# Modulation pieces of a linear-attention layer as VectorE row sums, gate logits ahead of one projection unit, and the next block's low part ahead of the norm's root

## The reference

```
m = einsum('bd,de->be', silu(c), w_ada) + b_ada          # 6 x 1024 values per layer and group
sh1, sc1, gt1, sh2, sc2, gt2 = split(m, 6)
h = rms_norm(x, norm) * (1 + sc1) + sh1
x = x + gt1 * gla_mixer(h)        # q, k, v, r, gate logits -> chunkwise state -> out
x = x + gt2 * conv_ffn(rms_norm(x, norm) * (1 + sc2) + sh2)
```

## Time and profile before

| | us |
|---|---|
| median of 3 runs (lowest, highest) | 1480.11 (1478.75, 1481.41) |
| the profiled execution | 1480.64 |
| its span | 1478.9 |
| TensorE busy | 1426.8 (96%) |
| VectorE busy | 830.7 (56%) |
| ScalarE busy | 644.9 (44%) |
| mean granted TensorE clock | 0.994 |

### The profile page before, as it was taken

One profiled execution on the slowest core, in us unless ns is written; L12 is line 12 of the kernel. 1 busy time (PEld: TensorE's weight loads), 2 busy tenths in 40 slices (PEclk: granted clock), 3 DMA queues, 4 the chain that ended last, 5 costly groups with the idle time before them and its releaser, 6 DMA issues.

```text
span 1478.9 us, 27109 instructions
## 1 busy us (share of the span) xinstructions
PE 1426.8 (96%) x11464; PEld 1328.3 (90%) x11464; DVE 830.7 (56%) x1332; ACT 644.9 (44%) x1427; POOL 78.9 (5%) x122
## 2 busy tenths in 40 slices
PE   4999999999999999999989999999899999999999
PEld 2877788899999999999978887878799999999999
DVE  4533442537776866868654455465675555455454
ACT  4423433436555245243354655553455552452431
POOL 0000000030000000000210000000200000000000
PEclk9999999999999999999999999999999999999999
DMA  9233242253333533534532232212512222223222
GB/s 376 92 140 124 88 154 93 93 200 115 114 115 103 183 121 109 172 121 152 215 118 87 74 100 74 65 49 77 200 58 86 86 72 100 86 72 103 84 74 103
DMA packets 34074, 171.87 MB, mean 116 GB/s; under 512 B 3857, under 2 KB 6033, under 8 KB 22050
## 3 DMA queue, kind: packets, MB, share of 16 engines
q1 hardware_dynamic: 21330, 118.49, 22.7%
q0 software_dynamic: 12624, 51.66, 9.5%
HBM read 162.22 MB, written 7.91 MB: 115 GB/s over the span
## 4 chain that ended last, share of the span: by engine, by line
PE 91%; DVE 4%; ACT 2%; issue 1%; DMA 1%; POOL 1%; POOLq 0%; SPq 0%; DVEq 0%; ACTq 0%
PE ps L548 27%; PE ps L550 26%; PE ps L549 26%; PE ps L649 1%; PE ps L921 1%; PE ps L963 1%; DVE w_lo L1432 1%; PE ps L586 1%; DVE h_lo L1481 1%; PE ps L876 1%; POOL acc L481 1%; DVE sq L1474 1%; PE ps L656 1%; ACT w_hi L1022 1%; PE ps L941 1%
## 5 line engine op out<-in xcount | busy, mean ns | idle before, releaser
L548 PE MATMUL ps<-h_hi,w_hi 128*128 128x272 f32 x2080 | 609.5, 293 | 12.4 <-DVE h_lo L1481 10.3
L550 PE MATMUL ps<-h_hi,w_lo 128*128 128x272 f32 x2080 | 603.4, 290 | 0.0
L549 PE MATMUL ps<-h_lo,w_hi 128*128 128x272 f32 x2080 | 600.4, 289 | 0.0
L548 PEld LDWEIGHTS ps<-h_hi,w_hi 128*128 128x128 f32 x2080 | 393.2, 189 | 24.6 <-issue 12.7
L549 PEld LDWEIGHTS ps<-h_lo,w_hi 128*128 128x128 f32 x2080 | 394.0, 189 | 1.2 <-issue 1.2
L550 PEld LDWEIGHTS ps<-h_hi,w_lo 128*128 128x128 f32 x2080 | 392.8, 189 | 0.0
L1432 DVE TENSOR_TENSOR w_lo<-w_raw,w_hi 128x2048 fp32r<-128x2048 f32 (+2 forms) x109 | 227.1, 2083 | 113.7 <-ACT w_hi L1022 113.5
L1022 ACT CAST w_hi<-w_raw 128x2048 fp32r<-128x2048 f32 (+2 forms) x109 | 188.2, 1727 | 217.2 <-PE ps L550 182.4
L549 PE MATMUL ps<-act_lo,w_hi 128*128 128x272 f32 (+1 forms) x704 | 204.1, 290 | 0.0
L548 PE MATMUL ps<-act_hi,w_hi 128*128 128x272 f32 (+1 forms) x704 | 203.6, 289 | 0.0
L550 PE MATMUL ps<-act_hi,w_lo 128*128 128x272 f32 (+1 forms) x704 | 203.4, 289 | 0.0
(11 more groups left out here) (250 smaller groups left out, 1612.1 us busy)
## 6 DMA issues: line engine op xcount, KB each, us to landing
w_raw<-in_wst SPq DMA_DIRECT2D x73, 1024.0 KB, 4.8
w_raw<-in_wst SPq DMA_DIRECT2D x28, 768.0 KB, 4.1
a_raw<-in_ada_r POOLq DMA_DIRECT2D x32, 512.5 KB, 3.7
a_raw<-in_ada_w POOLq DMA_DIRECT2D x24, 512.0 KB, 5.0
a_gap<-in_ada_w POOLq DMA_DIRECT2D x12, 1024.0 KB, 8.6
a_pro<-in_ada_w SPq DMA_DIRECT2D x8, 1024.0 KB, 18.5
w_raw<-in_wst SPq DMA_DIRECT2D x8, 512.0 KB, 3.7
xT<-in_xT SPq DMA_DIRECT2D x4, 544.0 KB, 7.7
```

The lines of the kernel that those rows point to most:

```text
L548: mm(out, lhs_hi, rhs_hi, start=first, stop=False)
L549: mm(out, lhs_hi, rhs_lo, start=False, stop=False)
L550: return mm(out, lhs_lo, rhs_hi, start=False, stop=last)
```

## The change

Five things change.

1. The pieces 8 to 19 become row sums: 48 instructions of 128 x 1024 on VectorE, twelve in each head slot, placed by the table `GLA_ROWS` (its entry says how many follow the units of a fill step). The 12 products on TensorE, the 12 copies on ScalarE, the 12 selections and the 12 additions go. One addition of all biases (`gla_biases`) comes at the end of the last slot. GpSimd loads rows (`ada_g`, the same bytes, a half at a time, each after the row sums that last read that half) and, once, the two rows of `c` spread over the partitions into `a_part` and `sq`; ScalarE applies silu to them, with a table load before and after.
2. `GLA_STEPS` has seven steps: one unit moves from before the gate logits to between the logits and the second pair of states. In the first and the last slot the step ahead of `turn_outputs` has one unit in place of two.
3. ScalarE squares a head's output in place in PSUM, after its copy, so that `sq` is free.
4. At the three boundary norms, `low` of the next block stands ahead of the wait for the root.
5. There, the product of the fourth piece moves from before the first chunk to after the second, into bank 6 in place of 7; the copy of the third piece waits for it as well.

```diff
@@ head slots on TensorE @@
-                rider = 8 + 3 * h
+                def fill(step):
+                    units([next(todo) for _ in range(GLA_STEPS[h][step])])
                 fill(0)
                 keys_and_scores(h)
                 fill(1)
-                ada_mm(rider)
                 state_terms(h, 0)
-                fill(2, rider)
-                ada_mm(rider + 1)
+                fill(2)
                 ...
-                fill(3, rider + 1)
+                fill(3)
                 ...
                 gate_logits(h + 1)
-                ada_mm(rider + 2)
+                fill(4)
                 state_terms(h, 1)
@@ tables @@
-GLA_STEPS = [[1, 3, 2, 1, 1, 1], [1, 3, 2, 2, 2, 3], [1, 3, 2, 2, 2, 3], [1, 3, 2, 1, 0, 1]]
+GLA_STEPS = [[1, 3, 1, 1, 1, 1, 1], [1, 3, 2, 1, 1, 2, 3], [1, 3, 2, 1, 1, 2, 3], [1, 3, 1, 1, 1, 0, 1]]
+GLA_ROWS = [[0, 3, 3, 0, 2, 2, 2], [1, 3, 2, 0, 2, 2, 2], [1, 3, 2, 0, 2, 2, 2], [2, 3, 3, 0, 2, 2, 0]]
@@ head slots on VectorE @@
+                def fill(step_):
+                    rows = GLA_ROWS[h][step_]
+                    for _ in range(GLA_STEPS[h][step_]):
+                        evacuate(next(todo), not (h == GH - 1 and step_ == 6))
+                        if rows:
+                            ada_rows()
+                            rows -= 1
+                    for _ in range(rows):
+                        ada_rows()
@@ one row sum @@
+                gla = m < GLA_ROWS_DONE
+                x = a_raw[:, t, 0:D] if gla else a_raw[:, t, :]
+                c = c_gla[grp] if gla else c_row[:, grp, :]
+                STT(out=prod_gla if gla else a_prod[:, :], in0=x, scalar=1.0, in1=c, op0=ALU.mult, op1=ALU.mult,
                     accum_out=ada[:, l, 2 * b + t, grp:grp + 1]).then_inc(arow_ok, 1)
+            def gla_biases():
+                dve.wait_ge(arow_ok, GLA_ROWS_DONE)
+                TT(ada[:, 0, t, :], ada[:, 0, t, :], b_ada[...], ALU.add).then_inc(bias_ok, 1)
@@ loads, on GpSimd @@
+                    if n < len(GLA_RIDERS):
+                        pool.dma_start(a_raw[:, t, 0:D], A["ada_g"][n, t]).then_inc(a_in[t], 16)
@@ ScalarE, an output of a head @@
-                A_(sq[0:m, 0, 0:DV], ps[0:m, b, 0:DV], ACT.Square, accum_out=o_ss[0:m, r:r + 1])
-                act.copy(o_rows[0:m, r, :], ps[0:m, b, 0:DV]).then_inc(o_out, 1)
+                act.copy(o_rows[0:m, r, :], ps[0:m, b, 0:DV])
+                A_(ps[0:m, b, 0:DV], ps[0:m, b, 0:DV], ACT.Square, accum_out=o_ss[0:m, r:r + 1]).then_inc(o_out, 1)
@@ ScalarE, before the first slot @@
+            act.wait_ge(crow_in, 32)
+            for grp in range(2):
+                A_(c_gla[grp], c_gla[grp], ACT.Silu).then_inc(crow_ok, 1)
+            act.preload_act_table_set(LNEXP)
@@ a boundary norm, VectorE @@
             def norm(which, n_ada):
                 make_gain(which, (0, KT), n_ada)
+                low(BN[{1: ("up", 0, 0, 1), 2: ("dq", 0), 3: ("up", 1, 0, 1)}[which]])
                 dve.wait_ge(rstd_ok, which + 1)
                 ...
                     modulated_lo(which, k)
-                    if k == 3:
-                        low(BN[{1: ("up", 0, 0, 1), 2: ("dq", 0), 3: ("up", 1, 0, 1)}[which]])
@@ a boundary norm, TensorE @@
                 ada_mm(riders[2])
-                ada_mm(riders[3])
 
             def first_after(which, name, stage):
-                first_block(name, stage, range(0, 6))
+                first_block(name, stage, range(0, 2))
+                ada_mm(riders[3])
+                first_block(name, stage, range(2, 6))
```

More of the change, by code:

```diff
@@ L54 @@
 GAP_RIDERS = {1: list(range(20, 24)), 2: list(range(40, 44)), 3: list(range(44, 48))}
-RAW_NO = {i: n for n, i in enumerate(GLA_RIDERS + FFN_RIDERS)}
+ROW_RIDERS = GLA_RIDERS + FFN_RIDERS
 GAP_NO = {i: n for n, i in enumerate(GAP_RIDERS[1] + GAP_RIDERS[2] + GAP_RIDERS[3])}
-ROWS_DONE = 4 * len(FFN_RIDERS)
+GLA_ROWS_DONE, ROWS_DONE = 4 * len(GLA_RIDERS), 4 * len(ROW_RIDERS)
 DC = D + 1
-ada_count = lambda i: i + 1 if i < FFN_RIDERS[0] else i + 1 - len(FFN_RIDERS)
+ada_count = lambda i: i + 1 - sum(j <= i for j in ROW_RIDERS)
+GLA_ROWS = [[0, 3, 3, 0, 2, 2, 2], [1, 3, 2, 0, 2, 2, 2], [1, 3, 2, 0, 2, 2, 2], [2, 3, 3, 0, 2, 2, 0]]
 VEC = {}
@@ L457, in _ @@
             pool.memset(eps[:, :], EPS).then_inc(const_ok, 1)
[L459 to L465, removed]
             def row_load(n):
@@ L504, in gap_loads @@
                     pool.dma_start(a_gap[:, GAP_NO[i] % 4, :, :], A["ada_w"][l, b].rearrange("p (k c) -> p k c", c=BC)).then_inc(a_gap_in[GAP_NO[i] % 4], 16)
-            for i in GLA_RIDERS:
-                rider_load(i)
+            pool.wait_ge(ada_mm_ok, 6)
+            row_load(0)
+            pool.wait_ge(ada_sel_ok, 8)
+            pool.wait_ge(h_ok, KT)
+            for grp in range(2):
+                pool.dma_start(c_gla[grp], A["c_row"][grp:grp + 1].partition_broadcast(P)).then_inc(crow_in, 16)
+            for n in range(1, len(GLA_RIDERS)):
+                row_load(n)
             pool.wait_ge(h_ok, 2 * KT)
@@ L512, in _ @@
             sum_tiles(1)
-            pool.wait_ge(ada_mm_ok, GAP_RIDERS[1][-1] + 1)
+            pool.wait_ge(ada_mm_ok, ada_count(GAP_RIDERS[1][-1]))
             pool.dma_start(c_row[:, :, 0:D], A["c_row"].partition_broadcast(P)).then_inc(crow_in, 16)
             pool.memset(c_row[:, :, D:DC], 1.0).then_inc(crow_one, 1)
-            for n in range(len(FFN_RIDERS)):
+            for n in range(len(GLA_RIDERS), len(ROW_RIDERS)):
                 row_load(n)
@@ L628, in ada_mm @@
                     src = lambda k: a_pro[:, i, k, :]
-                elif i in GAP_NO:
+                else:
                     pe.wait_ge(a_gap_in[GAP_NO[i] % 4], 16 * (GAP_NO[i] // 4 + 1))
                     src = lambda k: a_gap[:, GAP_NO[i] % 4, k, :]
[L632 to L635, removed]
                 if i in GAP_NO:
@@ L1052, in part @@
             def part(i):
-                act.wait_ge(ada_mm_ok, ada_count(i))
+                act.wait_ge(ada_mm_ok, ada_count(i) + (1 if i in GAP_NO and GAP_NO[i] % 4 == 2 else 0))
                 if i >= 4:
@@ L1169, in gla_slot @@
                     act.preload_act_table_set(LNEXP)
-                part(rider)
                 fill(2)
-                part(rider + 1)
                 fill(3)
                 gates(h + 1)
-                part(rider + 2)
+                fill(4)
                 outputs_out(h, 0, 6)
@@ L1462, in make_gain @@
                 dve.wait_ge(ada_ok, ada_count(n_ada - 1))
-                if which >= 2:
-                    dve.wait_ge(arow_ok, ROWS_DONE)
+                if which:
+                    dve.wait_ge(arow_ok, ROWS_DONE if which >= 2 else GLA_ROWS_DONE)
+                if which == 1:
+                    dve.wait_ge(bias_ok, 1)
                 k0, k1 = ks
@@ L1662, in gla_slot @@
                 todo = iter(fill_units(h))
-                rider = 8 + 3 * h
-                def fill(step_, piece=None):
-                    n = GLA_STEPS[h][step_]
-                    for i in range(n):
-                        evacuate(next(todo))
-                        if piece is not None and i == (n - 1 if step_ == 4 else 0):
-                            ada_add(piece)
-                    if piece is not None and n == 0:
-                        ada_add(piece)
+                def fill(step_):
[7 more added lines that the diff above has]
+                        ada_rows()
                 fill(0)
@@ L1690, in gla_slot @@
                 else:
-                    evacuate(next(todo), False)
+                    fill(6)
+                    gla_biases()
                     output_lo(oT, 1, 0)
@@ L1959, in _layout @@
     A["ada_r"] = rows
+    A["ada_g"] = np.stack([f("w_ada")[0][:, i * BC:(i + 1) * BC].T.reshape(2, P, D) for i in GLA_RIDERS])
     vec = np.zeros((P, NVEC), np.float32)
```

48 lines of the change are left out of this document (27 added, 21 removed).

## The result

The changed kernel takes 1462.9 us in the median of four runs (1459.7 to 1464.9), against 1480.2 for the kernel before (four runs, one more than in the table above). The ratio is 0.988, with a 95% interval of 0.986 to 0.990: 17.3 us faster, well beyond the 3 us that can be told from nothing. The forecast was 1464.8. The profiled execution took 1464.41 us (span 1462.5), against 1480.64 before.

A forecast was written before the change was run, and what follows sets the result against it. TensorE was taken to bound the kernel (91% of the chain). 24.7 removed - 9.85 waits - 3.0 clock + 3.5 norms = 15.3 us off 1480.64: 1465.3 profiled, 1464.8 as median; range 1454 to 1470.

The forecast's parts named there:

- Removed, 24.7: Linear-attention part, TensorE: products 12.0, selections 5.4, idle time 5.8 and slow clock after the first slot's hole 1.5 us go.
- The 1.7 us ahead of the outputs: TensorE's idle time before the outputs, waiting for VectorE's `bb`; claimed to go because a projection unit now covers it.
- Waits, 9.85: New TensorE waits for VectorE's queue across the four head slots: 4.35 + 0.2 + 4.4 + 0.9 us.
- The two of 0.1: Second and third slot, TensorE's wait for the gated output: 0.1 us counted in each.
- The 0.9 us of the first slot: First slot's new TensorE waits: 0.15 us at the third v unit, 0.75 at the second states.
- rival (a): VectorE gets through its stream earlier, so the new linear-attention waits don't form: 1452 us; chance 0.13.
- Clock, 3.0: Slow clock behind new linear-attention holes: 1.5 us for the 4.35 us hole, half that for each of two of 2.2.
- Rival (c): TensorE's clock stays at 2.4 GHz through the new holes; 3.0 and 2.5 us come back: 1459 us; chance 0.18.
- Norms, 3.5: Three boundary norms: net gain of 0.6 + 2.2 + 0.7 us from the earlier low part, slow stretches charged.
- Row sums, 1.22: VectorE's time per new row sum, from the profile's row for 1025 elements; 1.25 us taken with its semaphore.
- rival (b): A row sum takes 2.44 us in the head slots: +24 us, 1489, slower than before; chance 0.04.
- Rival (d): Row-sum loads are late, at 7.6 us: 2.1 us more in the first slot, about 1 later: 1468 us; chance 0.15.

## Why the prediction was right

The profiled time was foretold as 1465.3 and came as 1464.41; 1.6 us of the difference to before is the wait for the first inputs, so that the change itself gave 14.6 where the sum said 15.3. By the medians it gave 17.3, 1462.9 for 1464.8. The mechanism was right at the places that carry the sum (work removed, waits and their releasers, slow stretches behind them), but the closeness of the sum is luck in part: in the profiled execution the waits came 1.85 us shorter and the clock cost some 2 more, and at the norms two wrong sizes cancel.

**Removed, 24.7.** The stage lost 11.4 us while it took on 8.0 of holes and 4.7 of slow clock: 24.1 were removed. The total was right; one term had the wrong label. The 1.7 us ahead of the outputs is not what the moved logits are worth. The product that stood there had covered part of VectorE's gates, and without it the old order has waits of 0.6, 1.85 and 1.85, one of 1.1 at a v unit of the first slot, 0.3 more, and slow stretches: 8.9 us in all. The prediction compared with a state in which both edits were made, so the error in the label did no harm.

**Waits, 9.85.** The gated output: 4.35 walked, 4.21 measured. The third v unit: 2.2 walked, 1.91 measured, twice, with the releaser named. The two of 0.1 are not in the trace. The 0.9 us of the first slot didn't appear: the gate logits' unit, the second states (L758 at 96.34) and the v units follow one another there without a wait. Sum 8.0. This was the boldest part and carried rival (a) away: the moved row sums show that exactly these waits, and nothing else of 60 us of new VectorE work, stood on the path.

**Clock, 3.0.** 4.7 in the profiled execution, where all three holes were followed by a slow stretch. But this was chance in part: with the same holes, five other executions kept full speed behind both of 1.91 us, and lost (1 - clock) x 8 us = 1.7 to 2.5 behind the one of 4.2. The changed kernel's own runs show it too: the fastest, 1459.7 us, had a mean clock of 0.994, the others (1461.4, 1464.4, 1464.9) 0.991; 1461.4 and 1464.9 at one clock show that not all of the spread is the clock's. So the term is 2 to 5 us, and 3.0 was a mean of things that either happen or don't, which I had read off two holes of 2.08 us. Rival (c) is half true: it held for ten of twelve holes of 1.91 us, and not for the long one in any of six executions. The spare matmuls show, for the holes at the norms, that the hole causes the slow stretch: with them it is absent six times of six, without them it is there 17 times of 18.

**Norms, 3.5.** 3.3 measured. The split by edit, 0.6, 2.2 and 0.7, was as well: 0.6, 1.95 and 0.7. The second norm's share rests on a slow stretch that the execution of before had by chance; with the edit undone the three were alike. Two sizes in this term were off. The slow stretch behind the 3.45 us hole costs 1.3 us and not 0.6, by the seven spare matmuls. And with the clock kept the edit is worth 2.0 us a norm (21.0, 21.6, 21.6 against 19.0, 19.6, 19.6), where the prediction had 1.3 at the third. There 1.3 less 0.6 and 2.0 less 1.3 are both 0.7: the two errors cancel. The "6" that the prediction gives for the clock kept is these 2.0 three times, but its own terms don't give it: 3.5 and the two charges of 0.6 are 4.7.

**Row sums, 1.22.** As the earlier trace rows had it. That refutes rival (b), and the Trainium skill's rule (Vector Engine (DVE) Microarchitecture Reference, "Points that are easy to get wrong"), read as a doubling, doesn't hold for this instruction here: 48 of 1024 fp32 elements with both inputs in SBUF and a sum taken, 1.20 to 1.23 us. That is 1.19 ns an element, against 1.12 for the low part, which has two such inputs and takes no sum (2048 elements in 2.29 us). The rival's price was too low, though: 1501 and not 1489, for the clock.

**Loads and silu.** 22 loads in the stretch landed in 3.4 to 6.1 us, median 3.5, and no row sum waited for one. Rival (d) didn't come up. The two table loads and the two silu took ScalarE 4.6 us (68.32 to 72.92); the split behind them began 2.2 us later after the first gate logits than before, and TensorE didn't wait for it.

## What to carry to other kernels

Work moved to an idle engine is priced by its place in that engine's queue, not by its sum. Walk the queue from the event that releases it to the next thing that the bounding engine waits for, and put the work where the idle time is: 60 us of it cost 11.3 us at one set of places and less than 1 us at another. Where a piece of work is removed, ask what it had been covering; an ordering edit may be worth nothing or 9 us, by what stands around it. Price a hole on TensorE with a slow stretch behind it, and where it can't be closed, move real work into it, or even spare matmuls. Then look again at what bounds the stretch: at the norms two savings of over 1 us each give little more together than one alone, because VectorE is next in line.

## What the runs showed of the hardware

Whether TensorE slows down behind a short hole differs between holes of the same length, and the cost doesn't follow the length. Behind 1.91 us there was nothing ten times and 1.7 us lost twice, both in one execution; behind 1.85 us, ahead of the outputs, a slow stretch four times of four; behind 2.6 us four times of six; behind 3.45 and 3.52 us at the norms 17 times of 18, in six kernels (not at the first norm of the kernel with moved row sums); behind 4.2 us six times of six (1.7 to 2.5 us lost). In the kernel with doubled row sums, holes of 3.7 to 6.4 us were followed by 2.6 to 3.0 us lost, and the one of 9.29 by 1.5. What decides between them stays open; no run separated it.

An fp32 matmul stands as two rows in the trace: the 12 spare ones are 24 rows in 5.45 us, so 0.45 each. I had read the column sums' four rows in 1.08 us as four matmuls of 0.27; they are two of 0.54. The same count gives a piece's product 8 matmuls, not 16.
